# Seven-product stage, its first pairs: VectorE's order around pair one, and T1's low half on GpSimd

## The chip, the cores and the metric

The kernel runs on one core of one Trainium2 chip. The metric is the device time of one execution in microseconds. The engines are TensorE (PE in the profile; PEld is its weight load), VectorE (DVE), ScalarE (ACT), GpSimd (POOL) and SyncE (SP), which issues the loads.

## What is computed

Two layers of a decoder trunk on 512 tokens of width 1024, in float32. Each has token mixing (three branches), a LayerNorm, and then the stage that the change touches: a SwiGLU feed-forward network of hidden width 2816, together with a gate for an embedding of the layer.

```python
f_gate, f_up = jnp.split(x @ w_ffn_in, 2, axis=-1)
ffn = (jax.nn.silu(f_gate) * f_up) @ w_ffn_out
ple = jax.nn.sigmoid(x @ w_ple_gate) * (p_i @ w_ple_proj)
return layer_norm(ALPHA * x + ffn + ple, ln2_g, ln2_b)
```

## The kernel before

**Numbers in two parts.** Every product is made of three TensorE passes on a high and a low part of each operand (function `three`, lines 1234 to 1236): high by high, high weights by low tokens, low weights by high tokens. ScalarE makes a high part by rounding, and VectorE or GpSimd makes the low part by subtracting it from the unrounded value.

**Ahead of the stage.** Two of the 22 feed-forward blocks are multiplied directly, as four projection tiles (`T_R` to `T_R + 3`). GpSimd makes the low halves of the first three; that of the last is made by VectorE ("tile low", line 2133), which signals `r_low`. At line 753 GpSimd waits for `r_low` and adds one to `lo_ready`, the count on which SP's loads wait (line 600). "Hidden" (lines 2156 and 2159) is the product of the two projections of a block.

**Seven products.** For the other blocks, two weight blocks at a time, the product of a 2x2 block matrix of weights with a 2x2 block matrix of tokens (upper and lower half of the width, first and second 256 tokens) is made with seven multiplications in place of eight. There are 24 such pairs: pairs 0 to 3 belong to the embedding's gate, the others to the feed-forward network. The text calls pair index 1 "pair one" and index 2 "pair two". One multiplication is a *unit* of twelve matmuls on 128x256. Four need sums of weights (s1 to s4; VectorE's "sum1" to "sum4", lines 2175 to 2193), and four take sums of tokens, T1 to T4, which are the same for all pairs and made once in a layer: "t" on VectorE (lines 2141 and 2143), "t high" on ScalarE (line 1140), "t low" on VectorE (line 2148 for T1 and T3, line 2150 for T2 and T4). T1 is the difference of two blocks of x; in unit 7 (s1 of pair 0) it is needed first.

The units of the first pairs run in this order: 0 a11.0, 1 a12.0, 2 a11.1, 3 a12.1, 4 s3.0, 5 s2.0, 6 a22.0, 7 s1.0, 8 s3.1, 9 s4.0, 10 s2.1, 11 a22.1, 12 s1.1, 13 a11.2, 14 s3.2, 15 s4.1, 16 s2.2, 17 a12.2, 18 a22.2, 19 s1.2, 20 a11.3, 21 s3.3, 22 s4.2 (the number behind the point is the pair's index).

**What a pair's results pass through.** ScalarE copies intermediate results out of PSUM (m1, m7, u2), VectorE adds them to the accumulators (c11 line 2201, c21 line 2207, c22 line 2218). For pairs 0 to 3 ScalarE then takes a Tanh of each token half, and VectorE multiplies with the embedding's projection ("product first" and "product second", line 2228) and adds to the residual `u` ("low first" and "low second", line 2236). "Low second" signals `gated`. Unit a11 of pair j (from j = 2 on) waits for `gated` of pair j - 2, unit s3 for c21 of the pair before, s4 for c22 of its own pair, s2 for m1 of its own pair, and a11 of index 1 for both blocks' "hidden".

**What sets the order.** `ffn_steps` (line 263) gives each of ScalarE, VectorE and GpSimd a list of steps, each with a number, and sorts it; the numbers are counted in units, and an engine works through its list in order. A step that waits holds everything behind it on that engine. VectorE's low halves of unit i stand at i - 3.5, and its step "low" is line 2129. GpSimd makes the low halves of the units a11, a12 and a22 (line 757).

Of the kernel before, what the change touches and what calls it, by code (L numbers as in the profile page):

```python
# [19 lines left out]
ALU = mybir.AluOpType  # L20
ACT = mybir.ActivationFunctionType
F32 = mybir.dt.float32
# [234 lines left out]
R_BANKS = ((2, 3), (1, 4))  # L257
T3, T2, T4, T1 = 1, 2, 3, 0
T_MADE = {T1: 1, T3: 2, T2: 3, T4: 4}
T_HIGHS, T_LOWS = (T1, T3, T2, T4), (T3, T2, T1, T4)  # L260


def ffn_steps():

    act = [(-9.1, ("t high", T1)), (-9, ("t high", T3)), (-8.9, ("t high", T2)), (-8.8, ("gate", 0)), (-4.4, ("gate", 1)),
           (2.4, ("t high", T4)), (19, ("hidden high", 0)), (26, ("hidden high", 1))]
    dve = [(-9.1, ("t", T1)), (-9, ("t", T3)), (-8.95, ("t", T2)), (-8.9, ("tile low", T_R + 3)), (-8.8, ("t low", T3)),
           (-8.7, ("t low", T2)), (-8.6, ("hidden", 0)), (-6, ("sum3", 0)), (-4.6, ("sum1", 0)), (-4, ("sum2", 0)),
           (-3.9, ("sum4", 0)), (0.55, ("hidden", 1)), (1.6, ("t", T4)), (2.1, ("t low", T1)), (3.2, ("t low", T4)),
           (3.55, ("sum3", 1)), (3.6, ("sum1", 1)), (5.6, ("sum2", 1)), (1.55, ("c11", 0)), (10.5, ("c11", 1)),  # L270
           (20, ("hidden low", 0)), (27, ("hidden low", 1))]
    pool = []
    for i, (kind, j) in enumerate(FFN_UNITS):
        act.append((i - (6 if kind in ("a12", "a22") else 5) + 0.5, ("high", i)))
        if kind not in ("a11", "a12", "a22"):
            dve.append((i - 4 + 0.5, ("low", i)))
    for j in range(NS):
        at = {kind: UNIT_AT[(kind, j)] for kind in PRODUCT}
        late = 1 if j < NG else 0
        act += [(at["a11"] + 1, ("m1", j)), (at["s3"] + 1 if j else 3.45, ("m7", j)),  # L280
                (at["s2"] + 1 if j else 5.45, ("u2", j)),
                (at["a22"] + 2 if j < NG else at["a12"] + 2, ("th first", j)), (at["s4"] + 1, ("th second", j))]
        if j >= NG:
            act += [(at["a22"] + 3, ("high first", j)), (at["s4"] + 3, ("high second", j))]
        if j > 1:
            dve.append((at["a12"] + 1, ("c11", j)))
        dve += [(at["a22"] + 1 if j else 5.55, ("c21", j)), (at["s1"] + 1 if j else 6.45, ("c22", j)),
                (at["a22"] + 2 + late, ("product first", j)), (at["a22"] + 4, ("low first", j)),
                (at["s4"] + (1.6 if late else 2), ("product second", j)),
                (at["s4"] + (2.4 if late else 4), ("low second", j))]  # L290
        if j:
            dve.append((at["a11"] - 0.4 if j > 1 else at["s4"] - 8.4, ("sum4", j)))
        if j >= 2:
            dve.append((at["s2"] - 6, ("sum2", j)))
        pool += [(at[kind] - 5, ("low", at[kind])) for kind in ("a11", "a12", "a22")]
        if j >= 2:
            dve += [(at["a11"] - 6, ("sum3", j)), (at["a11"] - 4.4, ("sum1", j))]
    act += [(NU - 6 + 0.6, ("tile", 0)), (NU - 4 + 0.6, ("tile", 1)), (NU - 2 + 0.6, ("tile", 2))]
    return [sorted(steps, key=lambda step: step[0]) for steps in (act, dve, pool)]
# [63 lines left out]
def build(nc, x_t, ple_t, pos, freq, weights, params, out):  # L363
    with ExitStack() as ctx:
# [168 lines left out]
        raw2_loaded = [sem("raw2_loaded0"), sem("raw2_loaded1")]  # L533
        x_raw = sem("x_raw")
        r_low = sem("r_low")
        t_made, t_high, t_low = sem("t_made"), sem("t_high"), sem("t_low")
        unit_high, unit_low, unit_used = sem("unit_high"), sem("unit_low"), sem("unit_used")
        a11_low = sem("a11_low")
        sum1, sum3, sum2, sum4 = sem("sum1"), sem("sum3"), sem("sum2"), sem("sum4")
# [112 lines left out]
        def _(pool):  # L652
# [50 lines left out]
            for layer in range(L):  # L703
# [43 lines left out]
                tiles(layer, T_OUT, T_R)  # L747
                for t in range(T_R, T_S - 1):
                    low(t, first)
                pool.wait_ge(r_low, layer + 1)  # L750
                pool.wait_ge(lo_ready, first + (T_S - 1))
                for _ in range(1):
# [478 lines left out]
        def _(pe):  # L1231
# [268 lines left out]
            for layer in range(L):  # L1500
# [88 lines left out]
                def unit(i):  # L1589

                    kind, j = FFN_UNITS[i]
                    at = layer * NS + j
                    source, k0, token = PRODUCT[kind]
                    if kind in ("a12", "a22"):
                        arrived(T_S + TILE_UNIT_AT[(kind, j)], first)
                    elif kind == "a11":
                        pe.wait_ge(a11_low, at + 1)
                    else:
                        pe.wait_ge(unit_low, layer * NLOW + (LOW_UNIT_AT[(kind, j)] + 1))
                    if j == 0 and source == "t":  # L1600
                        pe.wait_ge(t_low, layer * 4 + (T_LOWS.index(k0) + 1))
                    if kind == "a11" and j == 1:
                        pe.wait_ge(ffn_s, layer * NR + NR)
                    elif kind == "a11" and j >= NG + 2:
                        pe.wait_ge(h_done, layer * FK + (NR + j - 2 - NG + 1))
                    elif kind == "a11" and j >= 2:
                        pe.wait_ge(gated, layer * NG + (j - 1))
                    elif kind == "s3":
                        if j == 0:
                            pe.wait_ge(ffn_s, layer * NR + 1)  # L1610
                        else:
                            pe.wait_ge(c21_ready, at)
                    elif kind == "s4":
                        pe.wait_ge(c22_ready, at + 1)
                    elif kind == "s2":
                        pe.wait_ge(m1_copied, at + 1)
                    elif kind == "a12":
                        if j == 0:
                            pe.wait_ge(ffn_s, layer * NR + 1)
                        else:  # L1620
                            pe.wait_ge(c11_ready, at)
                    elif kind == "a22":
                        pe.wait_ge(m7_copied, at + 1)
                    elif kind == "s1":
                        pe.wait_ge(u2_copied, at + 1)
                    bank = {"a12": B_BANK, "s3": E_BANK, "a22": E_BANK}.get(kind, A_BANK[j % 2])
                    onto = kind not in ("a11", "a12", "s3")
                    for k in range(KH):
                        if source == "x":
                            tok_h, tok_l = xh[:, k0 + k, token:token + HALF], xl[:, k0 + k, token:token + HALF]  # L1630
                        else:
                            tok_h, tok_l = t_hi[:, k0, k], t_lo[:, k0, k]
                        c = slice(k * P, k * P + P)
                        last = three(psum[:, bank, 0:HALF], ring(wh, i)[:, c], ring(wl, i)[:, c], tok_h, tok_l,
                                     k == 0 and not onto, k == KH - 1, onto)
                    last.then_inc(unit_used, 1)
# [740 lines left out]
```

## Time and profile before

| | |
|---|---|
| median of 3 runs | 1766.08 us (1764.22 to 1767.32) |
| the profiled execution | 1764.14 us, span 1762.3 us |
| TensorE busy | 1741.4 us (99%) |
| VectorE busy | 1268.4 us (72%) |
| ScalarE busy | 968.5 us (55%) |
| GpSimd busy | 892.2 us (51%) |
| granted TensorE clock, mean | 0.998 of full speed |

The shares are means over many stages. In a timeline row the first number is the start in us from the start of the span, the second the duration; a number in brackets at the end is the idle time of the engine just before, with what ended it. The stage stands twice in the trace; the rows below are of the first layer, where its first unit starts at 507.90 us.

### The profile page before, as it was taken

The numbers are of one execution on the slowest core, as the hardware profiler recorded it, in microseconds if no ns is written. First come the engines' busy times: TensorE is split into PE (matmuls) and PEld (weight loads), VectorE is DVE, ScalarE is ACT, GpSimd is POOL, SyncE is SP. The second block draws the span as 40 slices with busy tenths as digits, with TensorE's granted clock in tenths as the row PEclk, the third lists the DMA queues.
The fourth block names the chain that finished last, engine by engine and source line by source line (L and its number), as shares of the span: only waits on it lengthen the run. The fifth ranks groups of instructions, "written<-read, shape, count | busy, mean of one in ns | idle before, by whom it ended". The sixth has DMA issues, their size and how long they took to land.

```text
span 1762.3 us, 29278 instructions
## 1 busy us (share of the span) xinstructions
PE 1741.4 (99%) x10142; PEld 1532.9 (87%) x10142; DVE 1268.4 (72%) x2457; ACT 968.5 (55%) x1909; POOL 892.2 (51%) x522
## 2 busy tenths in 40 slices
PE   9999999999999999999999999999999999999997
PEld 8878888888789999988898788888887899999886
DVE  6279889877799888713363888897868998886033
ACT  4545887844466555522244558877445655655222
POOL 5446779654433343454434566895544343334542
PEclk9999999999999999999999999999999999999999
DMA  5334221223333223233223333212232323232331
GB/s 182 97 95 122 82 74 61 73 84 102 95 115 113 104 97 120 74 122 104 96 88 97 106 107 91 68 61 79 89 103 89 120 97 119 98 102 93 118 104 64
DMA packets 50411, 171.93 MB, mean 98 GB/s; under 512 B 6240, under 2 KB 6496, under 8 KB 50272
## 3 DMA queue, kind: packets, MB, share of 16 engines
q1 hardware_dynamic: 49408, 168.84, 30.2%
q8 instruction: 82, 1.34, 0.3%
q10 hardware_dynamic: 864, 1.28, 0.2%
q14 instruction: 57, 0.47, 0.1%
HBM read 162.76 MB, written 2.10 MB: 94 GB/s over the span
## 4 chain that ended last, share of the span: by engine, by line
PE 93%; DVE 4%; ACT 2%; issue 1%; DMA 0%; SPq 0%; DVEq 0%; ACTq 0%
PE banks L1234 25%; PE banks L1236 25%; PE banks L1235 25%; PE banks L1291 3%; PE banks L1293 3%; PE banks L1292 3%; PE banks L1403 2%; PE banks L1359 2%; DVE sb_xl L1936 1%; DVE sb_u L1929 1%; PE banks L1390 1%; DVE sb_u L1899 1%; PE banks L1383 1%; PE banks L1323 1%; PE banks L1384 1%
## 5 line engine op out<-in xcount | busy, mean ns | idle before, releaser
L669 POOL TENSOR_TENSOR sb_wl<-sb_wraw,sb_wh 128x1024 fp32r<-128x1024 f32 x205 | 497.6, 2431 | 500.3 <-ACT sb_wh L813 474.7
L1234 PE MATMUL banks<-sb_xh,sb_wh 128*128 128x512 f32 (+1 forms) x1152 | 403.7, 350 | 5.3 <-DVE sb_u L2236 3.5
L1236 PE MATMUL banks<-sb_xh,sb_wl 128*128 128x512 f32 (+1 forms) x1152 | 389.2, 338 | 0.0
L1235 PE MATMUL banks<-sb_xl,sb_wh 128*128 128x512 f32 (+1 forms) x1152 | 388.5, 337 | 0.0
L813 ACT ACTIVATE sb_wh<-sb_wraw 128x1024 fp32r<-128x1024 f32 x199 | 210.3, 1058 | 260.5 <-PE banks L1236 151.4
L1234 PEld LDWEIGHTS banks<-sb_xh,sb_wh 128*128 128x128 f32 x1152 | 219.1, 190 | 26.8 <-issue 7.1
L1236 PEld LDWEIGHTS banks<-sb_xh,sb_wl 128*128 128x128 f32 x1152 | 218.7, 190 | 24.2
L1235 PEld LDWEIGHTS banks<-sb_xl,sb_wh 128*128 128x128 f32 x1152 | 219.5, 191 | 14.1
L1234 PE MATMUL banks<-sb_t_hi,sb_wh 128*128 128x256 f32 x768 | 217.3, 283 | 0.0
L1235 PE MATMUL banks<-sb_t_lo,sb_wh 128*128 128x256 f32 x768 | 217.3, 283 | 0.0
L1236 PE MATMUL banks<-sb_t_hi,sb_wl 128*128 128x256 f32 x768 | 217.3, 283 | 0.0
L757 POOL TENSOR_TENSOR sb_wl<-sb_wraw,sb_wh 128x512 fp32r<-128x512 f32 x72 | 94.0, 1319 | 156.6 <-ACT sb_wh L1132 156.6
L1848 DVE TENSOR_TENSOR sb_u<-sb_u,banks 128x512 f32<-128x512 f32 x32 | 21.9, 686 | 197.1 <-PE banks L1236 197.1
L1234 PEld LDWEIGHTS banks<-sb_t_hi,sb_wh 128*128 128x128 f32 x768 | 147.5, 192 | 0.0
L1235 PEld LDWEIGHTS banks<-sb_t_lo,sb_wh 128*128 128x128 f32 x768 | 147.5, 192 | 0.0
L1236 PEld LDWEIGHTS banks<-sb_t_hi,sb_wl 128*128 128x128 f32 x768 | 147.5, 192 | 0.0
L1795 DVE SCALAR_TENSOR_TENSOR banks<-sb_hconv,sb_par,banks 128x512 f32<-128x512 f32 x192 | 142.5, 742 | 0.5
L1234 PE MATMUL banks<-sb_hh,sb_wh 128*128 128x512 f32 x352 | 137.8, 391 | 0.0
L1235 PE MATMUL banks<-sb_hl,sb_wh 128*128 128x512 f32 x352 | 137.0, 389 | 0.0
L1236 PE MATMUL banks<-sb_hh,sb_wl 128*128 128x512 f32 x352 | 137.0, 389 | 0.0
L757 POOL TENSOR_TENSOR sb_wl<-sb_wraw2b,sb_wh 128x512 fp32r<-128x512 f32 x48 | 62.1, 1294 | 90.8 <-ACT sb_wh L1132 90.8
L2129 DVE TENSOR_TENSOR sb_wl<-banks,sb_wh 128x512 fp32r<-128x512 f32 x144 | 98.4, 683 | 2.3 <-ACT sb_wh L1132 2.3
(353 smaller groups left out, 4085.9 us busy)
## 6 DMA issues: line engine op xcount, KB each, us to landing
sb_wraw<-in_weights SPq DMA_DIRECT2D x256, 512.0 KB, 3.5
sb_wraw2a<-in_weights SPq DMA_DIRECT2D x24, 512.0 KB, 3.6
sb_wraw2b<-in_weights SPq DMA_DIRECT2D x24, 512.0 KB, 4.5
sb_u<-in_x SPq DMA_DIRECT2D x8, 256.0 KB, 6.5
sb_q_raw<-sb_qn_t SPq DMA_DIRECT2D x16, 128.0 KB, 2.2
sb_k_raw<-sb_kn_t SPq DMA_DIRECT2D x16, 128.0 KB, 2.3
out<-sb_u SPq DMA_DIRECT2D x8, 256.0 KB, 2.1
sb_q_raw<-sb_qr_t SPq DMA_DIRECT2D x16, 64.0 KB, 2.0
```

Source lines behind the costliest of these rows:

```text
L669: nc.gpsimd.tensor_tensor(wl[:, t % WS, :], wraw[:, t % 2, :], wh[:, t % WS, :].bitcast(F32), ALU.subtract).then_inc(lo_ready, 1)
L757: nc.gpsimd.tensor_tensor(ring(wl, n), raw_unit(kind, j), ring(wh, n).bitcast(F32), ALU.subtract).then_inc(a11_low if kind == "a11" else l ...
L813: nc.scalar.activation(wh[:, t % WS, :], wraw[:, t % 2, :], ACT.Copy).then_inc(hi_ready, 1)
L1234: nc.tensor.matmul(out, wh_, xh_, start=start, stop=False, skip_group_check=onto)
L1235: nc.tensor.matmul(out, wh_, xl_, start=False, stop=False, skip_group_check=onto)
L1236: return nc.tensor.matmul(out, wl_, xh_, start=False, stop=stop, skip_group_check=onto)
L1291: nc.tensor.matmul(o, th_, h[:, kk], start=(k == 0), stop=False)
L1292: nc.tensor.matmul(o, th_, lw[:, kk], start=False, stop=False)
L1293: last = nc.tensor.matmul(o, tl_, h[:, kk], start=False, stop=(k == GROUP_K[name] - 1))
L1359: last = nc.tensor.transpose(psum[0:rows, bank, b * P:b * P + P], src, ident[:])
L1795: steps.done(v.scalar_tensor_tensor(acc, h, w, acc, ALU.mult, ALU.add))
L2129: v.tensor_tensor(ring(wl, n), raw_unit(kind, j), ring(wh, n).bitcast(F32), ALU.subtract).then_inc(unit_low, 1)
```

## The change

Three things change, and all stand in the head of the stage.

In VectorE's list for pair 0, "product second", "low first" and "low second" move up to stand right behind "product first". Pair one's c11, c21 and c22, the low half of unit 15 (s4.1) and the weight sum "sum2" of pair two follow in a new order.

T1's low half ("t low" of T1) leaves VectorE's list. GpSimd makes it, ahead of its wait at line 753, as soon as ScalarE has rounded T1; it signals a semaphore of its own, `t1_low`, for which the unit s1.0 waits.

The other token sums' semaphore `t_low` therefore counts three in a layer in place of four.

```diff
-T_HIGHS, T_LOWS = (T1, T3, T2, T4), (T3, T2, T1, T4)
+T_HIGHS, T_LOWS = (T1, T3, T2, T4), (T3, T2, T4)
...
-            dve.append((i - 4 + 0.5, ("low", i)))
+            dve.append((i - 4 + 0.5 if i != UNIT_AT[("s4", 1)] else 10.54, ("low", i)))
...
                 for t in range(T_R, T_S - 1):
                     low(t, first)
+                pool.wait_ge(t_high, layer * 4 + (T_HIGHS.index(T1) + 1))
+                nc.gpsimd.tensor_tensor(t_lo[:, T1], t_raw[:, T1], t_hi[:, T1].bitcast(F32), ALU.subtract).then_inc(t1_low, 1)
                 pool.wait_ge(r_low, layer + 1)
                 pool.wait_ge(lo_ready, first + (T_S - 1))
...
-                        pe.wait_ge(t_low, layer * 4 + (T_LOWS.index(k0) + 1))
+                        if k0 == T1:
+                            pe.wait_ge(t1_low, layer + 1)
+                        else:
+                            pe.wait_ge(t_low, layer * 3 + (T_LOWS.index(k0) + 1))
```

VectorE from "product first" of pair 0 to c22 of pair one, before (`banks` is PSUM; line 2228 is a product, 2236 an addition to `u`, 2187 a "sum2" and 2193 a "sum4", 2129 a low half, 2201, 2207 and 2218 are c11, c21 and c22):

```order
L2228 SCALAR_TENSOR_TENSOR banks<-banks,sb_pp 128x512
L2236 SCALAR_TENSOR_TENSOR sb_u<-sb_u,banks 128x2x256
L2187 TENSOR_TENSOR banks<-banks,sb_wraw 128x512
L2201 TENSOR_TENSOR banks<-banks,sb_m_126 128x256
L2129 TENSOR_TENSOR sb_wl<-sb_wl_raw,sb_wh 128x512
L2228 SCALAR_TENSOR_TENSOR banks<-banks,sb_pp 128x512
L2236 SCALAR_TENSOR_TENSOR sb_u<-sb_u,banks 128x2x256
L2129 TENSOR_TENSOR sb_wl<-banks,sb_wh 128x512
L2207 SCALAR_TENSOR_TENSOR banks<-banks,sb_u_128 128x256
L2129 TENSOR_TENSOR sb_wl<-banks,sb_wh 128x512
L2193 TENSOR_TENSOR banks<-banks,sb_wraw 128x512
L2218 SCALAR_TENSOR_TENSOR banks<-banks,sb_m_127 128x256
```

And now (lines stand six further down):

```order
L2234 SCALAR_TENSOR_TENSOR banks<-banks,sb_pp 128x512 x2
L2242 SCALAR_TENSOR_TENSOR sb_u<-sb_u,banks 128x2x256 x2
L2135 TENSOR_TENSOR sb_wl<-sb_wl_raw,sb_wh 128x512
L2207 TENSOR_TENSOR banks<-banks,sb_m_126 128x256
L2213 SCALAR_TENSOR_TENSOR banks<-banks,sb_u_128 128x256
L2135 TENSOR_TENSOR sb_wl<-banks,sb_wh 128x512
L2193 TENSOR_TENSOR banks<-banks,sb_wraw 128x512
L2224 SCALAR_TENSOR_TENSOR banks<-banks,sb_m_127 128x256
L2135 TENSOR_TENSOR sb_wl<-banks,sb_wh 128x512
L2199 TENSOR_TENSOR banks<-banks,sb_wraw 128x512
```

Both products and both additions stand first; "sum2" of pair two has gone from the third place to the ninth instruction, and c22 ahead of the last low half.

GpSimd from the last projection tiles to its first units, before (line 669 is a tile's low half, 757 a unit's):

```order
L669 TENSOR_TENSOR sb_wl<-sb_wraw,sb_wh 128x1024 x3
L757 TENSOR_TENSOR sb_wl<-sb_wraw,sb_wh 128x512 x2
L757 TENSOR_TENSOR sb_wl<-sb_wraw2b,sb_wh 128x512
L757 TENSOR_TENSOR sb_wl<-sb_wraw2a,sb_wh 128x512
L757 TENSOR_TENSOR sb_wl<-sb_wraw,sb_wh 128x512
```

And now:

```order
L670 TENSOR_TENSOR sb_wl<-sb_wraw,sb_wh 128x1024 x3
L752 TENSOR_TENSOR sb_t_lo<-sb_t_raw,sb_t_hi 128x1024
L760 TENSOR_TENSOR sb_wl<-sb_wraw,sb_wh 128x512 x2
L760 TENSOR_TENSOR sb_wl<-sb_wraw2b,sb_wh 128x512
L760 TENSOR_TENSOR sb_wl<-sb_wraw2a,sb_wh 128x512
```

T1's low half stands between the tiles' and the units' low halves, ahead of the signal to the loads.

## Rows read from the trace of the kernel before

**Rows 1.** The page, part 1: busy time, share of the span, instructions.

```profile
PE 1741.4 (99%) x10142; PEld 1532.9 (87%) x10142; DVE 1268.4 (72%) x2457; ACT 968.5 (55%) x1909; POOL 892.2 (51%) x522
```

**Rows 2.** Waits of TensorE, whole span: us in total, times, longest.

```profile
PE banks L1234 <- DVE sb_u L2236: 3.5, 2, 1.7
```

**Rows 3.** Timeline, TensorE, unit 12 to 13: start, us, line, names, idle before.

```profile
526.49 0.28 PE L1236 MATMUL banks<-sb_t_hi,sb_wl 128*128 128x256 f32 x1
528.52 0.36 PE L1234 MATMUL banks<-sb_xh,sb_wh 128*128 128x256 f32 x1 [1.75 <-DVE sb_u L2236]
```

**Rows 4.** Timeline, VectorE, around unit 13.

```profile
523.96 0.69 DVE L2228 SCALAR_TENSOR_TENSOR banks<-banks,sb_pp 128x512 f32<-128x512 f32 x1
524.75 0.69 DVE L2236 SCALAR_TENSOR_TENSOR sb_u<-sb_u,banks 128x512 f32<-128x512 f32 x1
525.35 0.69 DVE L2187 TENSOR_TENSOR banks<-banks,sb_wraw 128x512 f32<-128x512 f32 x1
...
527.68 0.69 DVE L2236 SCALAR_TENSOR_TENSOR sb_u<-sb_u,banks 128x512 f32<-128x512 f32 x1
...
529.22 0.68 DVE L2129 TENSOR_TENSOR sb_wl<-banks,sb_wh 128x512 fp32r<-128x512 f32 x1
```

**Rows 5.** Timeline, ScalarE, the same stretch.

```profile
522.96 0.59 ACT L1170 ACTIVATE banks<-banks 128x512 f32<-128x512 f32 x1
...
526.14 0.60 ACT L1132 ACTIVATE sb_wh<-banks 128x512 fp32r<-128x512 f32 x1 [1.81 <-DVE banks L2187]
526.63 1.14 ACT L1132 ACTIVATE sb_wh<-sb_wraw 128x512 fp32r<-128x512 f32 x2
```

**Rows 6.** Timeline, GpSimd and VectorE, a few units later.

```profile
527.33 2.52 POOL L757 TENSOR_TENSOR sb_wl<-sb_wraw,sb_wh 128x512 fp32r<-128x512 f32 x2 [3.85 <-ACT sb_wh L1132]
...
533.25 1.24 DVE L2180 TENSOR_TENSOR banks<-sb_wraw2b,sb_wraw2a 128x512 f32<-128x512 f32 x1
```

**Rows 7.** Timeline, VectorE's c22 of pair two and TensorE's unit 22.

```profile
540.01 0.42 DVE L2218 SCALAR_TENSOR_TENSOR banks<-banks,sb_m 128x256 f32<-128x256 f32 x1
...
541.54 0.28 PE L1234 MATMUL banks<-sb_xh,sb_wh 128*128 128x256 f32 x1
```

**Rows 8.** Timeline, ScalarE and VectorE, the token sums.

```profile
496.82 1.05 ACT L1140 ACTIVATE sb_t_hi<-sb_t_raw 128x1024 fp32r<-128x1024 f32 x1
...
497.33 1.22 DVE L2141 TENSOR_TENSOR sb_t_raw<-sb_u,sb_t_raw 128x1024 f32<-128x1024 f32 x1
498.48 1.22 DVE L2133 TENSOR_TENSOR sb_wl<-sb_wraw,sb_wh 128x1024 fp32r<-128x1024 f32 x1
...
512.47 1.21 DVE L2148 TENSOR_TENSOR sb_t_lo<-sb_t_raw,sb_t_hi 128x1024 fp32r<-128x1024 f32 x1
...
512.58 1.06 ACT L1140 ACTIVATE sb_t_hi<-sb_t_raw 128x1024 fp32r<-128x1024 f32 x1 [2.66 <-DVE sb_t_raw L2143]
```

**Rows 9.** Timeline, GpSimd and VectorE in earlier stages.

```profile
401.52 2.43 POOL L669 TENSOR_TENSOR sb_wl<-sb_wraw,sb_wh 128x1024 fp32r<-128x1024 f32 x1 [2.17 <-ACT sb_wh L813]
401.62 2.88 DVE L2062 TENSOR_TENSOR sb_gb<-sb_gb,sb_ga 128x512 f32<-128x512 f32 x1
...
125.53 3.05 POOL L669 TENSOR_TENSOR sb_wl<-sb_wraw,sb_wh 128x1024 fp32r<-128x1024 f32 x1 [2.49 <-ACT sb_wh L813]
```

**Rows 10.** TensorE, SP's waits, ScalarE and VectorE ahead of unit 2.

```profile
502.46 0.39 PE L1234 MATMUL banks<-sb_xh,sb_wh 128*128 128x512 f32 x1
...
SPq L600 <- POOLq L753: 7.1, 1, 7.1
...
506.09 0.63 ACT L1132 ACTIVATE sb_wh<-sb_wraw2b 128x512 fp32r<-128x512 f32 x1 [0.90 <-DMA sb_wraw2b<-in_weights]
...
507.79 1.26 DVE L2129 TENSOR_TENSOR sb_wl<-sb_wl_raw,sb_wh 128x512 fp32r<-128x512 f32 x1 [1.48 <-ACT sb_wh L1132]
...
509.68 0.69 DVE L2159 TENSOR_TENSOR sb_th<-sb_th,banks 128x512 f32<-128x512 f32 x1
...
510.77 0.28 PE L1234 MATMUL banks<-sb_xh,sb_wh 128*128 128x256 f32 x1
```

More of the change, by code:

```diff
@@ L268, in ffn_steps @@
            (-8.7, ("t low", T2)), (-8.6, ("hidden", 0)), (-6, ("sum3", 0)), (-4.6, ("sum1", 0)), (-4, ("sum2", 0)),
-           (-3.9, ("sum4", 0)), (0.55, ("hidden", 1)), (1.6, ("t", T4)), (2.1, ("t low", T1)), (3.2, ("t low", T4)),
-           (3.55, ("sum3", 1)), (3.6, ("sum1", 1)), (5.6, ("sum2", 1)), (1.55, ("c11", 0)), (10.5, ("c11", 1)),
+           (-3.9, ("sum4", 0)), (0.55, ("hidden", 1)), (1.6, ("t", T4)), (3.2, ("t low", T4)),
+           (3.55, ("sum3", 1)), (3.6, ("sum1", 1)), (5.6, ("sum2", 1)), (1.55, ("c11", 0)), (10.51, ("c11", 1)),
            (20, ("hidden low", 0)), (27, ("hidden low", 1))]
@@ L286, in ffn_steps @@
             dve.append((at["a12"] + 1, ("c11", j)))
[L287 to L290, printed above, removed]
+        dve += [({0: 5.55, 1: 10.52}.get(j, at["a22"] + 1), ("c21", j)),
+                ({0: 6.45, 1: 10.58}.get(j, at["s1"] + 1), ("c22", j)),
+                (at["a22"] + 2 + late, ("product first", j)), (at["a22"] + 4 if j else 9.5, ("low first", j)),
+                (at["s4"] + (1.6 if late else 2) if j else 9.3, ("product second", j)),
+                (at["s4"] + (2.4 if late else 4) if j else 9.7, ("low second", j))]
         if j:
@@ L293, in ffn_steps @@
         if j >= 2:
-            dve.append((at["s2"] - 6, ("sum2", j)))
+            dve.append((at["s2"] - 6 if j > 2 else 10.56, ("sum2", j)))
         pool += [(at[kind] - 5, ("low", at[kind])) for kind in ("a11", "a12", "a22")]
@@ L535, in build @@
         r_low = sem("r_low")
-        t_made, t_high, t_low = sem("t_made"), sem("t_high"), sem("t_low")
+        t_made, t_high, t_low, t1_low = sem("t_made"), sem("t_high"), sem("t_low"), sem("t1_low")
         unit_high, unit_low, unit_used = sem("unit_high"), sem("unit_low"), sem("unit_used")
```

## The prediction

> **What bounds the kernel now.** I read the page first: TensorE is busy for 99% of the span [rows 1], so only a stretch in which it stands still, or starts late, can change the time. The view of its waits, next, shows how little of that there is: the longest entry is 3.5 us in two waits, one in each layer, for VectorE's line 2236 [rows 2]. Line 2236 with the second token half is "low second", which signals `gated`; unit 13 of the stage (a11 of pair two) may not start without it. TensorE's timeline shows one such wait: the last matmul of unit 12 started at 526.49, the next could have started 0.12 us later, and it started at 528.52 after an idle stretch of 1.75 us [rows 3]. With the slower first matmuls behind it this costs about 1.95 us in a layer, 3.9 us in both. No edit to the order around pair one can win more than that.
>
> VectorE is the engine waited for. From 523.96 its rows follow each other without an idle entry [rows 4]; two independent operations on 512 columns start 0.60 us apart (524.75 and 525.35). So what is moved ahead moves something else back by as much. That is why the later waits matter: the last TensorE start that hangs on this row of work is unit 22 (s4 of pair two), at 541.54, and what it needs, c22 of pair two, ended at 540.01 + 0.42 = 540.43 [rows 7]. The hand-over from VectorE to TensorE took 0.15 us at the wait itself (527.68 + 0.69 = 528.37 to 528.52) [rows 3, 4]. Unit 22 thus had 541.54 - 540.58 = 0.96 us to spare. However early TensorE gets away at unit 13, it is stopped there again unless VectorE itself is earlier: **0.96 us, not 1.95, is the most that a new order can keep in a layer.**
>
> **The moved operations of pair one.** In the new order "product first", "product second", "low first" and "low second" follow each other from 523.96 at 0.60 us each. The Tanh that "product second" needs ended at 522.96 + 0.59 = 523.55 on ScalarE [rows 5], so it does not hold it. "Low second" starts at 525.76 and ends at 526.45 in place of 528.37, 1.92 us earlier. With 0.15 us for the hand-over TensorE is released at 526.60, when it is ready (526.61): the wait goes.
>
> What was put back is late next. The weight sum "sum2" of pair two started at 525.35 [rows 4]; in the new order it comes behind three 0.60 us operations (the other product and both additions take the place of one), the low half of s3, two 0.34 us copies of c11 and c21, and the low half of s4, and ends near 528.9, 2.9 us later. ScalarE waits for just that result (1.81 us idle before its row at 526.14) and has two more roundings (1.14 us for both), a Tanh and the copy of m1 queued behind it [rows 5]. At some 0.55 us each, from 529.0, m1 is copied by about 531.4. Unit 16 wants it at 526.61 + 3 x 1.44 = 530.93 (1.44 us is twelve matmuls at 0.12 us), so TensorE waits 0.5 to 0.6 us there. The low half that VectorE takes of this sum, at 529.22 before, must now wait for ScalarE until 529.6 (+0.4). And GpSimd's two low halves that started at 527.33 [rows 6] start near 530.2 and end near 532.8, across VectorE's weight sum "sum3" of pair three, which reads SBUF twice. By the blocking shown below this costs up to 1.3 us, less the 0.56 us that the sum at 533.25 (1.24 us, where 0.68 is usual) lost to GpSimd before and then no longer loses [rows 6]. VectorE reaches c22 of pair two some 0.8 us later than before, so unit 22 starts at 541.4 in place of 541.54. I take 0.1 us won in a layer from the new order; the ends are 0.96 us won and 0.4 us lost.
>
> **T1's low half.** The operation removed from VectorE takes 1.21 us at 512.47, but VectorE's next one needs T4's rounding, which ScalarE ends at 512.58 + 1.06 = 513.64 [rows 8], where the removed one ended at 513.68. Removing it gives VectorE nothing but an idle microsecond. What matters is where the operation goes. GpSimd is free then, and gets it when T1 is rounded, at 496.82 + 1.05 = 497.87. VectorE is at that moment inside T2 (497.33 for 1.22 us), and the low half of the last projection tile is next (498.48 to 499.70) [rows 8]; both have two SBUF inputs.
>
> How these two engines share SBUF is seen elsewhere in this trace: a GpSimd subtraction of the same size asked at 401.52 while a two-input VectorE operation ran; it was done by 403.95, and VectorE's following two-input operation, 0.68 us long when alone, took 2.88 us, from 401.62 until 0.55 us after GpSimd's end [rows 9]. That is 2.2 us lost. Where GpSimd asked as late as 0.2 us before VectorE's operation ended, VectorE's next one went first and GpSimd took 3.05 us [rows 9]. Here it asks at about 497.95, 0.6 us ahead of 498.55, so I take the first pattern: the tile's low half ends at 501.9, not 499.7. The Trainium skill, SBUF — State Buffer, section "Who interferes with whom", has it as a lock: a VectorE instruction with two SBUF inputs and a GpSimd one that reads SBUF block each other fully, and issue order decides who waits. The trace agrees, with 2.2 us for a 2.43 us instruction; the page's "whole instruction" would make it 2.4 us and the sum below 0.4 us larger.
>
> Three things hang on that low half. TensorE's projection of the tile started at 502.46 [rows 10]; 501.9 and 0.15 are still in time. GpSimd's signal at line 753 waits for it, and SP's load of the pair's second weight tile waits for line 753 (7.1 us) [rows 10], with the loads of pair one queued behind it. These loads are late by the same 2.2 us, since nothing else holds them: ScalarE stood 0.90 us for them at 506.09, and VectorE then 1.48 us for ScalarE at 507.79 [rows 10]. So VectorE's idle time does not absorb the delay; it moves with it. "Hidden" of the second block ended at 509.68 + 0.69 = 510.37 and ends at 512.57. Unit 2 (a11 of pair one), which waits for it, started at 510.77 [rows 10] and starts at 512.72: 1.95 us lost, and about 0.1 us more for the restart, as at unit 13.
>
> **Sum.** In each layer + 2.05 + 0.1 for VectorE, which stays the later of the two by that much, - 0.1 for the new order: 2.05 us; two layers, 4.1 us. The profiled execution took 1764.14 us (span 1762.3) and would take 1768.2. It lies 1.94 us under the median of the three runs, 1766.08, so the forecast on that scale is **1770.2 us**. The bounds for T1's move are 0 (GpSimd runs where VectorE reads PSUM) and 2.4 us plus 0.4 if the projection is held too; with the order's bounds a layer lies between -0.96 and +3.2.
>
> **The rivals.**
> 1. *T1's low half costs nothing and VectorE is relieved.* For it: 1.21 us leave an engine whose rows show no idle entry for long [rows 4]. Against it: VectorE's operations at 497.33 and 498.48 both read SBUF twice [rows 8], and its time at 512.47 was not on the path. The order's 0.1 us a layer is left: 1765.9. The Trainium skill, Perfetto Trace Analysis, section "Optimizing Scalar/DVE Operations", leaves both open: with a saturated VectorE moving work may pay, and between these two engines it might not, since they share a port.
> 2. *The tile's low half goes first, T1's behind it* (the 3.05 us pattern). Line 753 and the loads are then on time; the 2.2 us fall on the operations behind, where VectorE's idle 1.48 us takes part, and collisions with GpSimd's first four low halves give some back. "Hidden" would be 0.7 to 1.7 us late against 0.25 us of slack: 0.5 to 1.5 us a layer, near 1768.
> 3. *Faster.* T1 is free, and GpSimd's late low halves miss the sum of pair three: the 0.96 us of unit 22 are kept twice, 1764.2. To pass 0.2% a layer would have to win 1.8 us, which needs VectorE earlier at c22 than the trace has it.
> 4. *Slower still.* The tile's low half comes after 502.3 and holds the projection as well: from that point each microsecond counts fully; 0.5 us more in a layer, 1771.3.
>
> **How the numbers follow.** The forecast 0.62 (own range 1768.6 to 1771.5), rival 1 0.15, rival 2 0.10, rival 3 0.05, rival 4 0.08. A measurement here tells about 0.2%, 3.5 us, from no change: 1762.6 and 1769.6 are the lines. Of the forecast some 0.45 lies above the upper, with rival 4 0.53 slower; rival 3 passes the lower line in 0.03; the rest, 0.44, is the same. The range, 1765.6 to 1771.8, takes in rivals 1 and 2 and the upper part of 4.
>
> **What would show it.** Right: in the profile after, GpSimd's new row near 498 for 2.4 to 2.9 us, the tile's low half on VectorE near 3.4 us long in place of 1.22, line 753's signal near 501.9, a TensorE wait of 1.5 us or so for "hidden" at the stage's third unit, none at unit 13, and waits of about half a microsecond for m1 and for c22 of pair two. Wrong: the tile's low half still 1.2 us long, or TensorE without a wait at the third unit, or c22 of pair two earlier than now against unit 13.

## The result, and the profile after

The changed kernel takes 1768.38 us (median of 22 runs, 1768.00 to 1771.75), the kernel before in as many runs beside it 1765.78 us: a ratio of 1.0018, 95% interval 1.0012 to 1.0024. The change makes the kernel slower by 0.18%, clear of zero but under the 0.2% from which the prediction counted a change; by its own lines this is "the same". The forecast of 1770.2 us was 1.8 us too high: its own range, 1768.6 to 1771.5, missed the time by 0.2 us, and the whole range, 1765.6 to 1771.8, holds it. The profiled execution of the changed kernel took 1768.49 us (span 1766.7), which is 4.35 us more than that of before; the working had said 4.1 between these two.

In the trace after, line numbers above 750 are three higher on GpSimd, ScalarE and TensorE (753 is 756, 1234 is 1237), six higher on VectorE (2129 is 2135, 2228 is 2234, 2236 is 2242) and one higher on SP (600 is 601); those of the experiments lie in between. The page's first line, to be held against [rows 1]:

```profile
PE 1743.1 (99%) x10142; PEld 1532.8 (87%) x10142; DVE 1268.2 (72%) x2455; ACT 967.0 (55%) x1909; POOL 899.1 (51%) x524
```

Busy times tell nothing: two instructions went from VectorE to GpSimd, and the engines are as busy as before. The waits of TensorE tell it (us in total, times, longest):

```profile
PE banks L1237 <- DVE sb_th L2165: 2.7, 2, 1.3
...
PE banks L1237 <- DVE banks L2224: 1.2, 2, 0.6
PE banks L1237 <- ACT sb_m L1154: 1.2, 2, 0.7
...
PE banks L1237 <- POOL sb_wl L760: 0.5, 2, 0.3
```

The entry of [rows 2], 3.5 us for the second addition of pair one, is gone. Four others stand in its place, each twice, once in a layer. The timeline of TensorE, layer one, at units 0, 2, 13, 16 and 22 gives the starts:

```profile
508.54 0.39 PE L1237 MATMUL banks<-sb_xh,sb_wh 128*128 128x256 f32 x1 [0.21 <-POOL sb_wl L760]
...
513.01 0.36 PE L1237 MATMUL banks<-sb_xh,sb_wh 128*128 128x256 f32 x1 [1.33 <-DVE sb_th L2165]
...
528.92 0.35 PE L1237 MATMUL banks<-sb_xh,sb_wh 128*128 128x256 f32 x1
...
533.91 0.36 PE L1237 MATMUL banks<-sb_t_hi,sb_wh 128*128 128x256 f32 x1 [0.44 <-ACT sb_m L1154]
...
543.63 0.36 PE L1237 MATMUL banks<-sb_xh,sb_wh 128*128 128x256 f32 x1 [0.61 <-DVE banks L2224]
```

TensorE's starts in the two traces of before and after, set side by side, give what each unit lost (+) or won against the one listed above it, in us. The start of the program, long before the change, adds 0.3 us that belongs to the execution and not to the kernel.

| unit | layer one | layer two | waits for |
|---|---|---|---|
| 0 | +0.37 | +0.46 | GpSimd's first low half |
| 2 | +1.60 | +1.59 | "hidden" of the second block |
| 13 | -1.84 | -1.85 | nothing any more |
| 16 | +0.60 | +0.88 | m1 of pair two |
| 21 | +0.25 | +0.25 | c21 of pair two, and the slower restart in unit 16 |
| 22 | +0.83 | +0.84 | c22 of pair two |
| sum | +1.81 | +2.17 | |

Where the first two lines come from stands in the timelines of GpSimd and VectorE and in SP's waits:

```profile
498.24 2.88 POOL L752 TENSOR_TENSOR sb_t_lo<-sb_t_raw,sb_t_hi 128x1024 fp32r<-128x1024 f32 x1 [5.78 <-ACT sb_t_hi L1143]
...
497.63 1.23 DVE L2147 TENSOR_TENSOR sb_t_raw<-sb_u,sb_t_raw 128x1024 f32<-128x1024 f32 x1
498.77 3.42 DVE L2139 TENSOR_TENSOR sb_wl<-sb_wraw,sb_wh 128x1024 fp32r<-128x1024 f32 x1
...
SPq L601 <- POOLq L756: 18.6, 2, 9.3
```

GpSimd takes T1's low half at 498.24, while VectorE is inside T2; VectorE's low half of the projection tile, 1.22 us in [rows 8], takes 3.42 and ends at 502.19. SP then waits 9.3 us for GpSimd's signal in place of the 7.1 us of [rows 10], and the loads behind it are 2.2 us late.

### The profile page after: what moved, and what is told of

Read it like the earlier page. It is cut to its first block and busy times, and to the rows that moved or that the text cites. A ratio compares the mean times of both kernels' runs of the same rounds, so it can differ in the third digit from the quotient of the medians.

```text
span 1766.7 us, 29278 instructions
## 1 busy us (share of the span) xinstructions
PE 1743.1 (99%) x10142; PEld 1532.8 (87%) x10142; DVE 1268.2 (72%) x2455; ACT 967.0 (55%) x1909; POOL 899.1 (51%) x524
```

## The experiments

Ten kernels were run, nine of them 7 to 11 times each, beside fresh runs of the kernel before. What is compared first is the trace, unit by unit; the medians follow.

### The order alone

```diff
-T_HIGHS, T_LOWS = (T1, T3, T2, T4), (T3, T2, T4)
+T_HIGHS, T_LOWS = (T1, T3, T2, T4), (T3, T2, T1, T4)
...
-                nc.gpsimd.tensor_tensor(t_lo[:, T1], t_raw[:, T1], t_hi[:, T1].bitcast(F32), ALU.subtract).then_inc(t1_low, 1)
```

> The changed kernel with T1's low half back on VectorE, behind T2's (line 269 keeps the step "t low" of T1 and its key 2.1): the new order around pair one alone, the whole result computed. **Theory (the shared lock is the cost):** the order pays back what it takes. The wait of 1.95 us at unit 13 goes, and TensorE waits instead about 0.6 us at unit 16 for ScalarE's m1 and 0.6 to 0.7 us in all at units 21 and 22 for c21 and c22 of pair two; VectorE's add sum3 of pair two runs into GpSimd's lows and takes 1.5 us instead of 0.7, as it did in the changed kernel, and that is what makes c22 late. Net per layer between -0.7 and +0.1 us; median 1764.4 to 1766.0 us, 0 to -1.4 us against the kernel before. **Rival A (the order is the cost, T1's move is free):** the wait is given back in full and more; the kernel is as slow as the changed one, 1768.4 us. **Rival B (the order wins outright):** -1.9 us per layer with nothing new late at units 16 to 22; 1762.0 us.

Measured: 1764.38 us (1764.06 to 1764.87), ratio 0.9989 (0.9980 to 0.9998). TensorE's waits:

```profile
PE banks L1235 <- DVE banks L2219: 1.2, 2, 0.6
PE banks L1235 <- ACT sb_m L1152: 1.2, 2, 0.7
```

Against the trace of before, unit 13 starts 1.9 us earlier in each layer, and units 16, 21 and 22 give back 0.61 + 0.25 + 0.84 us in layer one and 0.88 + 0.24 + 0.84 in layer two. The order is worth nothing in the trace: 1764.24 us for the profiled execution, 1764.14 for that of before. Rivals A and B both fall. But the median is 1.5 us lower than before's, more than the trace explains; that difference is taken up below.

### T1's low half alone

```diff
+                pool.wait_ge(t_high, layer * 4 + (T_HIGHS.index(T1) + 1))
+                nc.gpsimd.tensor_tensor(t_lo[:, T1], t_raw[:, T1], t_hi[:, T1].bitcast(F32), ALU.subtract).then_inc(t1_low, 1)
```

> The kernel before with nothing but T1's low half moved to GpSimd, at line 751, ahead of the signal of line 753; VectorE's order around pair one is as before. The whole result is computed. **Theory (the shared lock is the cost):** VectorE's low half of the last token tile, ready to begin at 498.5 us, is held by GpSimd's add and ends near 502.2 instead of 499.7 us; through the semaphore of line 753 the loads into the token tile come 2.2 to 2.5 us later, hidden half 1 follows, and TensorE waits at unit 2 for it for 1.3 us more; unit 0 loses 0.3 to 0.4 us to GpSimd's first low half. The wait of 1.95 us at unit 13 stays, as a wait of about 1.9 us. Sum +1.6 to +2.3 us per layer, median 1769.0 to 1770.4 us, so slower than the changed kernel or level with it. **Rival A (T1's move is free or a relief to VectorE):** level with the kernel before, 1765.8 us or up to 1.2 us under it. **Rival B (T1's delay is absorbed by the wait at unit 13):** that wait shrinks from 1.95 to 0.3 us and the sum is +0.4 per layer, 1766.6 us.

Measured: 1770.24 us (1768.28 to 1771.75), ratio 1.0020 (1.0011 to 1.0029); the profiled execution 1768.28, 4.14 us over that of before. VectorE's row, then TensorE's waits:

```profile
498.55 3.42 DVE L2138 TENSOR_TENSOR sb_wl<-sb_wraw,sb_wh 128x1024 fp32r<-128x1024 f32 x1
```

```profile
PE banks L1236 <- DVE sb_u L2241: 3.6, 2, 1.8
PE banks L1236 <- DVE sb_th L2164: 2.7, 2, 1.3
...
PE banks L1236 <- POOL sb_wl L759: 0.5, 2, 0.3
```

Unit 0 is 0.37 and 0.42 us late, unit 2 another 1.59 in each layer, and the wait at unit 13 stays as it was: VectorE and TensorE are late by the same amount, so that wait takes nothing up. The theory holds; in the trace rival A is over 4 us off and rival B, with its 0.8 us for both layers, over 3. In the trace the two parts add: 0.1 for the order and 4.1 for T1 make 4.2, and the changed kernel's difference is 4.35.

### T1's low half behind the signal

```diff
-                pool.wait_ge(t_high, layer * 4 + (T_HIGHS.index(T1) + 1))
-                nc.gpsimd.tensor_tensor(t_lo[:, T1], ...).then_inc(t1_low, 1)
...
+                pool.wait_ge(t_high, layer * 4 + (T_HIGHS.index(T1) + 1))
+                nc.gpsimd.tensor_tensor(t_lo[:, T1], ...).then_inc(t1_low, 1)
```

The two lines move from ahead of the wait and signal of line 753 to right behind them.

> The changed kernel with T1's low half on GpSimd issued behind the signal of line 753 instead of ahead of it: GpSimd still does it at nearly the same time, but the loads into the token tile no longer wait for it in GpSimd's queue. The whole result is computed. **Theory 1 (what costs is GpSimd holding the memory that both engines use, whoever is next on VectorE):** the signal waits for the low half of the token tile, which now ends near 499.7 us, so the loads are on time and GpSimd's op begins right behind, at about 499.8 us; it then meets VectorE's next work (the first sums and lows of the stage) and the hidden half is late by 1 to 1.5 us by that road; TensorE waits at unit 2 for 1.0 to 1.4 us more than in the kernel before, unit 0 not at all. Per layer +1.0 to +1.5 with the order's 0 to -0.6: median 1766.6 to 1768.6 us. **Theory 2 (only the late signal of line 753 costs):** the loads are back at their time, hidden half 1 with them, unit 2 waits no longer than in the kernel before, and the median is that of the order alone, 1764.4 to 1766.0 us.

Measured: 1767.71 us (1766.76 to 1769.05), ratio 1.0009 (1.0000 to 1.0018). SP's wait, GpSimd's and VectorE's timelines, and TensorE's wait:

```profile
SPq L601 <- POOLq L754: 14.2, 2, 7.1
```

```profile
500.11 3.19 POOL L756 TENSOR_TENSOR sb_t_lo<-sb_t_raw,sb_t_hi 128x1024 fp32r<-128x1024 f32 x1 [7.74 <-POOLq L754]
```

```profile
498.69 1.22 DVE L2139 TENSOR_TENSOR sb_wl<-sb_wraw,sb_wh 128x1024 fp32r<-128x1024 f32 x1
499.83 1.22 DVE L2154 TENSOR_TENSOR sb_t_lo<-sb_t_raw,sb_t_hi 128x1024 fp32r<-128x1024 f32 x1
500.96 3.42 DVE L2156 SCALAR_TENSOR_TENSOR sb_t_lo<-sb_t_raw,sb_t_hi 128x1024 fp32r<-128x1024 f32 x1
...
506.23 1.78 DVE L2186 TENSOR_TENSOR banks<-sb_wraw 128x512 f32<-128x512 f32 x1
```

```profile
PE banks L1237 <- DVE sb_th L2165: 2.6, 2, 1.3
```

The signal is back at its time (7.1 us a layer, as in [rows 10]), the tile's low half takes 1.22 us again, and still TensorE waits 1.3 us at unit 2, which starts 1.47 us later than before. The 2.2 us have only moved on to VectorE's next operation, T2's low half: 3.42 us for 1.22. The idle 1.48 us that VectorE had ahead of 507.79 [rows 10] take up a part of them, and a weight sum that now runs beside GpSimd's first low halves, 1.78 us for 0.69, gives a part back. Theory 2 falls: the late signal is one road from the blocked operation to unit 2, not the cause. What the better place does save is unit 0, and some 0.5 us a layer in all.

### T1's low half 13 us later

```diff
+                    if n == UNIT_AT[("a22", 0)]:
+                        pool.wait_ge(t_high, layer * 4 + (T_HIGHS.index(T1) + 1))
+                        nc.gpsimd.tensor_tensor(t_lo[:, T1], ...).then_inc(t1_low, 1)
```

> The changed kernel with T1's low half on GpSimd behind the low half of unit 6, about 13 us later than in the changed kernel, when the loads, the tile's low half and the hidden half are long done. The whole result is computed; the operand is used first by a unit that comes later. **Theory (the place is the cost, not the engine):** the loads, hidden half 1 and units 0 and 2 are at the times of the kernel before; GpSimd's add of 2.4 us there holds VectorE's low of T4 by up to 1 us, and c21 of pair zero after it, so unit 8 waits some 0.3 us. Per layer +0.3 and the order's 0 to -0.6: median 1765.0 to 1766.6 us, level with the kernel before. **Rival (GpSimd is the wrong engine anywhere, its 2.4 us against VectorE's 1.2 us come back as a wait wherever it stands):** unit 8 or one of the next waits 1.2 us or more per layer, 1768 us or over.

Measured: 1766.30 us (1765.61 to 1766.61), ratio 1.0002 (0.9993 to 1.0011). GpSimd, VectorE and TensorE:

```profile
511.89 3.39 POOL L762 TENSOR_TENSOR sb_t_lo<-sb_t_raw,sb_t_hi 128x1024 fp32r<-128x1024 f32 x1
...
514.14 2.22 DVE L2157 SCALAR_TENSOR_TENSOR sb_t_lo<-sb_t_raw,sb_t_hi 128x1024 fp32r<-128x1024 f32 x1 [1.13 <-ACT sb_t_hi L1144]
...
519.19 0.36 PE L1238 MATMUL banks<-sb_t_hi,sb_wh 128*128 128x256 f32 x1 [0.64 <-ACT sb_u L1165]
```

Units 0 and 2 start as in the kernel before. The theory's size is right and its unit is wrong: T4's low half loses 1.00 us (2.22 for 1.22), the weight sum behind it comes later, ScalarE's rounding of that sum holds its copy of u2, and unit 7 waits and starts 0.79 us later in layer one and 0.80 in layer two, not unit 8 by 0.3. The cost of T1 on GpSimd falls from 2.1 to 0.9 us a layer by its place alone; at none of the three places did it become a gain, since the 1.2 us that it takes from VectorE were not on the path.

### Before once more, and one sum moved

The trace of before left two things open: why the order alone has a lower median than its trace gives, and what holds VectorE ahead of unit 13. The runs of before fall into three groups, 1.6 us apart, and each run's granted TensorE clock goes with them, in all but two of 74 runs (0.998 at 1766.38 and 1766.45 us, times of the middle group). All 22 runs of the two experiments without a long wait of TensorE, 1 and 4, kept 0.998.

> The kernel before once more, unchanged, for its trace. The 33 runs of it beside the first four experiments fall into three groups: ten at 1763.9 to 1764.7 us with a granted clock of 0.998 or 0.999, fifteen at 1765.5 to 1766.7 us, nearly all at 0.997, and eight at 1767.2 to 1768.0 us at 0.996 or 0.997; the trace at hand, 1764.14 us, is of the lowest. **Theory (the clock falls at the wait of 1.95 us before unit 13, in some executions, in one layer or in both):** if this execution is of a higher group, 1765.5 us or more, its trace shows TensorE's granted clock below 1.00 in the stretch behind unit 13 of one layer (two for 1767 and more), and 1.6 us more per layer there. **Rival:** the clock is 1.00 there and the time is lost elsewhere. An execution of the lowest group, 1763.9 to 1764.7 us, tells nothing on this.

It ran once, in 1764.64 us: the lowest group, which tells nothing on the clock. Its waits are those of before. What it does show is how far two executions of one kernel stand apart at the same clock: 0.5 us, all at the start of the program.

The second kernel changes one number in `ffn_steps`:

```diff
-            dve += [(at["a11"] - 6, ("sum3", j)), (at["a11"] - 4.4, ("sum1", j))]
+            dve += [(at["a11"] - 6 if j > 2 else 5.57, ("sum3", j)), (at["a11"] - 4.4, ("sum1", j))]
```

> The kernel before with one VectorE step moved: the weight sum sum3 of pair two goes from behind sum4 of pair one to behind c21 of pair zero, five places up. In the old place it meets GpSimd's low halves and runs 1.5 us; in the new one it does not. The whole result is computed. **Theory (VectorE's chain ahead of unit 13 is what TensorE waits for, and the length of that wait decides on the clock):** the wait at unit 13 falls from 1.95 to about 0.9 us in both layers and nothing else gets late: -0.9 us per layer, 1762.3 us for an execution with the clock at 0.998, and as no wait is as long as 1.9 us all runs lie in one group: median 1762.0 to 1762.8 us, 3.0 to 3.8 us under the median before. **Rival 1 (the groups do not come from that wait):** three groups as before, each 1.8 us lower, median 1764.0 us. **Rival 2 (sum3's time is not on the path):** unit 13 waits as before, 1765.9 us.

Measured: 1762.48 us (1762.02 to 1763.99), ratio 0.9981 (0.9972 to 0.9990). VectorE's row for the moved sum, and TensorE's wait at unit 13:

```profile
518.59 0.68 DVE L2175 TENSOR_TENSOR sb_wl_raw<-sb_wraw 128x512 f32<-128x512 f32 x1
```

```profile
PE banks L1234 <- DVE sb_u L2236: 1.8, 2, 0.9
```

The sum takes 0.68 us in its new place; in the old one it had taken 1.18, not the 1.5 that was expected. The wait is halved, from 1.75 us [rows 3] to 0.9. Unit 13 starts 0.80 and 0.90 us earlier in the two layers and nothing gives it back. The median falls by 3.3 us where the trace, 1760.6 against 1762.3 us of span, falls by 1.7. Rival 2 is out. Ten of the eleven runs have a granted clock of 0.998 and end by 1763.2; one, 1763.99, has 0.997. So of rival 1's three groups two are all but gone.

### The new order, mended

```diff
-            dve.append((at["s2"] - 6 if j > 2 else 10.56, ("sum2", j)))
+            dve.append((at["s2"] - 6 if j > 2 else 10, ("sum2", j)))
```

> The new order of the changed kernel with T1's low half on VectorE, as in the first experiment, and the weight sum sum2 of pair two put right behind pair one's second addition instead of behind c21 of pair one (its key 10 in place of 10.56). The whole result is computed. **Theory (the order gives its gain back because sum2 is put three places too late):** high half 16 on ScalarE, m1 of pair two, c21 and c22 of pair two are on time again: the waits at units 16, 21 and 22 go, unit 14 waits some 0.4 us for c21 of pair one. Net per layer about -1.3 us, median 1761.2 to 1762.0 us. **Rival (the wait moves on whatever the place: VectorE has no room in this stretch):** a wait of 0.6 us or more shows up again at units 13 to 22 in another place and the time is that of the first experiment, 1764.4 us.

Measured: 1761.35 us (1761.17 to 1761.86), ratio 0.9976 (0.9966 to 0.9986). The waits at units 16, 21 and 22 are gone, and one new entry is left, 0.35 us at unit 14 for c21 of pair one:

```profile
PE banks L1235 <- DVE banks L2208: 0.4, 2, 0.2
```

The rival falls. The give-back of the new order was no law of a full engine; it came from one step, "sum2" of pair two, put behind four operations, c11 and c21 of pair one and two low halves. With it ahead of them only c21 comes too late, by 0.35 us.

> The two moves together: the new order with sum2 of pair two right behind pair one's second addition, and sum3 of pair two behind c21 of pair zero; T1's low half on VectorE. The whole result is computed. **Theory:** no wait of TensorE over 0.1 us is left between units 8 and 40 of either layer, -1.9 us per layer against the trace of before: 1760.2 to 1761.0 us, all runs in one group, 4.8 to 5.6 us under the median before. **Rival (VectorE is near full here, a new collision with GpSimd's low halves takes the gain):** one of units 13 to 22 waits 0.5 us or more, 1761.5 to 1763 us.

This kernel has both edits, that of "sum2" and that of "sum3". Measured: 1760.88 us (1760.14 to 1761.17), ratio 0.9971 (0.9960 to 0.9982), the fastest of all here, 4.9 us under the kernel before and 7.5 under the changed one. The two stretches that held the wait at unit 13, in the trace of before and then in this one (length, then busy us and instructions of TensorE, its weight loads, VectorE, ScalarE and GpSimd, then granted clock, DMA share and GB/s):

```profile
526.00:545.00 19.00, 17.25 (x144) 17.08 (x143) 18.83 (x32) 11.99 (x25) 7.67 (x6) 1.00 0.33 114
1400.00:1420.00 20.00, 18.25 (x153) 18.08 (x152) 19.83 (x33) 13.01 (x27) 7.68 (x6) 1.00 0.32 107
```

```profile
526.00:545.00 19.00, 19.00 (x161) 19.00 (x160) 18.93 (x33) 13.17 (x27) 7.80 (x6) 1.00 0.35 120
1400.00:1420.00 20.00, 20.00 (x169) 20.00 (x169) 19.93 (x35) 13.66 (x28) 10.28 (x8) 1.00 0.31 107
```

TensorE, busy for 17.25 of 19 and 18.25 of 20 us before, does not stand still any more. The bound that the prediction gave for any order, 0.96 us a layer, does not hold: this order wins 1.97, and that of the seventh experiment won 1.49 and 1.39.

### A longer wait, and the sum of both parts

```diff
-                (at["s4"] + (2.4 if late else 4), ("low second", j))]
+                (at["s4"] + (2.4 if late else 4) if j else 12.55, ("low second", j))]
```

> The kernel before with VectorE's second addition of pair one moved three steps later, behind the low half of unit 16: the wait at unit 13 is made longer on purpose, from 1.95 to about 3.3 us. The whole result is computed. **Both theories:** the work alone is 1.3 to 1.5 us longer per layer, so an execution with the granted clock at 0.998 takes 1766.8 to 1767.4 us. **Theory (a longer wait at unit 13 lets the granted clock fall more often):** in the kernel before 17 of 54 runs kept their clock, with the wait at 0.9 us ten of eleven did, without it all; here fewer than 3 in 10 do, most runs are 1.6 us (one layer) or 3.2 us (both) above, 1768.5 to 1770.5 us, and the median is 1768.5 us or more. If the traced execution is one of them, the clock is below 1.00 right behind unit 13. **Rival (the groups have nothing to do with the length of this wait):** the share of the groups stays, about a third at the lowest, half 1.6 us above and a sixth 3.2 us above; the median is 1768.5 us too, and only the shares and the trace tell.

Measured: 1769.90 us (1767.92 to 1771.15), ratio 1.0024 (1.0015 to 1.0034). No run of ten has a granted clock of 0.998; two have 0.997, eight 0.996. The profiled execution is one of the two, and shows the thing itself. TensorE waits 3.07 us at unit 13 in both layers (6.1 us in two waits). In the first the clock stays; in the second it falls. The stretches by granted clock (third column from the end), layer one and layer two, each from the idle time on:

```profile
526.00:529.30 3.30, 0.30 (x3) 0.10 (x1) 3.30 (x7) 1.90 (x4) 2.42 (x2) 1.00 0.01 2
529.30:533.30 4.00, 3.92 (x33) 3.95 (x34) 3.55 (x7) 1.65 (x4) 0.07 (x1) 1.00 0.56 185
...
1401.00:1404.20 3.20, 0.32 (x3) 0.12 (x1) 3.20 (x7) 2.19 (x4) 2.03 (x2) 1.00 0.01 3
1404.20:1408.20 4.00, 3.81 (x20) 3.84 (x21) 2.81 (x7) 0.88 (x2) 0.47 (x1) 0.59 0.58 174
1408.20:1412.00 3.80, 3.80 (x33) 3.80 (x33) 2.22 (x5) 2.11 (x5) 1.30 (x1) 0.98 0.25 97
```

and TensorE's rows in layer two:

```profile
1404.39 0.36 PE L1234 MATMUL banks<-sb_xh,sb_wh 128*128 128x256 f32 x1 [3.07 <-DVE sb_u L2236]
...
1404.94 0.40 PE L1235 MATMUL banks<-sb_xl,sb_wh 128*128 128x256 f32 x1
1405.14 0.42 PE L1236 MATMUL banks<-sb_xh,sb_wl 128*128 128x256 f32 x1
1405.36 0.42 PE L1234 MATMUL banks<-sb_xh,sb_wh 128*128 128x256 f32 x1
...
1408.35 0.29 PE L1236 MATMUL banks<-sb_t_hi,sb_wl 128*128 128x256 f32 x1
```

From 1404.94 to 1408.35 matmuls start 0.21 us apart in place of 0.12, with the clock at the lower of its two levels (1.2 in place of 2.4 GHz); 16 starts at 0.09 us more each cost 1.5 us. That is the distance between the groups. The runs with a granted clock of 0.998 or more, by the longest idle time of TensorE in units 0 to 22:

| kernels | longest idle time | runs that kept 0.998 |
|---|---|---|
| experiments 1, 4, 6, 7, 8 | 0.9 us or less | 48 of 49 |
| the changed kernel, experiments 3 and 10 | 1.3 us | 37 of 44 |
| the kernel before | 1.75 us | 26 of 74 |
| experiment 2, with both waits | 1.79 us | 5 of 11 |
| this one | 3.07 us | 0 of 10 |

The rival, that the shares stay, falls. The length of the wait does not settle it alone: of the three kernels with 1.3 us the changed one kept its clock in 18 of 22 runs, experiment 3 in 8 of 11 and experiment 10 in all 11.

> The changed kernel, T1's low half on GpSimd ahead of the signal of line 753, with the two weight sums where the eighth experiment has them (sum2 of pair two behind pair one's second addition, sum3 behind c21 of pair zero). The whole result is computed. **Theory (the costs add: T1's low half on GpSimd costs the start of the stage, whatever VectorE's order is later):** against the eighth experiment unit 0 is 0.3 to 0.5 us and unit 2 another 1.6 us later in each layer, and no unit behind makes it good: +3.9 to +4.2 us, 1764.3 to 1765.0 us where the clock stays at 0.998. **Rival (the late start gives VectorE and GpSimd slack, and the good order then costs less than the sum):** unit 13 and those behind it start no more than 1.2 us late per layer, 1763.2 us or less.

Measured: 1764.81 us (1764.15 to 1765.08), ratio 0.9994 (0.9985 to 1.0003); the profiled execution 1764.37, 3.93 us over that of the eighth experiment, although the start of the program was 0.3 us shorter. Against that trace units 0 and 2 are 0.54 and 1.59 us late in layer one, 0.33 and 1.60 in layer two, and no unit behind waits; of the changed kernel's waits in the stage that for "hidden" and that for GpSimd's first low half are left:

```profile
PE banks L1237 <- DVE sb_th L2165: 2.7, 2, 1.3
...
PE banks L1237 <- POOL sb_wl L760: 0.5, 2, 0.4
```

The costs add. T1's low half costs 2.0 to 2.2 us a layer at the start of the stage, also with the better order of VectorE behind it; the rival falls.

## Why the prediction came out as it did

**The wait at unit 13 and what follows it.** Right. The two products came one behind the other at 526.30 and the two additions at 527.50, late by the 2 us that VectorE was late, and the wait went. VectorE's rows from there to c22:

```profile
526.30 1.28 DVE L2234 SCALAR_TENSOR_TENSOR banks<-banks,sb_pp 128x512 f32<-128x512 f32 x2
527.50 1.27 DVE L2242 SCALAR_TENSOR_TENSOR sb_u<-sb_u,banks 128x512 f32<-128x512 f32 x2
...
534.10 1.52 DVE L2181 TENSOR_TENSOR sb_wl_raw<-sb_wraw2b,sb_wraw2a 128x512 f32<-128x512 f32 x1
...
536.86 0.70 DVE L2186 TENSOR_TENSOR banks<-sb_wraw2b,sb_wraw2a 128x512 f32<-128x512 f32 x1
...
543.06 0.42 DVE L2224 SCALAR_TENSOR_TENSOR banks<-banks,sb_m 128x256 f32<-128x256 f32 x1
```

What gives it back is what the working named: m1 at unit 16 (0.60 and 0.88 us; 0.5 to 0.6 was said), and c22 at unit 22. The collision of "sum3" of pair three with GpSimd's two low halves is there, 1.52 us for 0.68, and the sum at 536.86 is free of it, as forecast, in place of the 1.24 us of [rows 6]. The 0.25 us up to unit 21 were not in the working; they are a part of the same delay: c21 ended at 541.21, and the unit started 0.15 us later, at 541.36. Net -0.16 and +0.12 us in the two layers, where 0.1 won was taken.

**T1's low half.** Right in place, road and size. The tile's low half ended at 502.19 (501.9 was said; the program's start adds 0.3), 3.42 us long, and did not hold the projection; 2.05 us were forecast up to unit 2, and units 0 and 2 together lost 1.97 and 2.05. One thing on the road was not named: the late loads also hold GpSimd's first low half, so 0.4 us of it fall at unit 0 already. Of the lock the Trainium skill, SBUF — State Buffer, section "Who interferes with whom", says that the port pair which both engines share is an exclusive lock, and that issue order decides who blocks. The traces agree: the VectorE operation that followed lost 2.20 us in the changed kernel and in the third experiment (3.42 for 1.22) and 1.00 us in the fourth, where it came only 1.14 us ahead of GpSimd's end, and in all three it ended 1.07 or 1.08 us after GpSimd's row, which is nearly its own length.

**The sum against the profile, and then the median.** The sum, 1764.14 + 4.1 = 1768.2 us for a profiled execution, was 0.3 us off, the 0.3 us of the program's start. The last step failed: "on that scale" I added 1.94 us, the distance of the profiled execution from the median, as if that belonged to every kernel. It does not. In about two of three executions of the kernel before (48 of 74) the granted clock falls, in 15 of them twice by their times, for 1.5 to 1.6 us each, and the experiments that shorten, remove or lengthen the wait of 1.75 us at unit 13 tie the fall to it; the traced executions happened to be free of it. The change takes that wait away and has one of 1.3 us at unit 2 instead, and most of the extra is gone: 18 of its 22 runs lie within 0.5 us of 1768.5, the other four, at 1770.6 to 1771.75 us with a clock of 0.996 or 0.997, pay. So the median moved by 2.6 us and the trace by 4.35. In the kernel with T1's part alone, which keeps the wait, the medians move by 4.4 and the traces by 4.14. The term that was mis-sized is this one: it should have been about zero (the changed kernel's median lies 0.1 us under its profiled execution). With it went the chances, which put "slower" (0.53) ahead of "the same" (0.44). The fall itself was caught only in the trace with the longer wait; that it is the same in the kernel before rests on the run times, their distance and the clock that each run reports, not on a trace. Why one execution keeps its clock and the next does not is open.

**The bound on any order.** The prediction said that 0.96 us is the most that a new order can keep in a layer, since TensorE is stopped at unit 22 "again unless VectorE itself is earlier". VectorE could be. Two of its sums ahead of unit 13 ran into GpSimd in the trace of before, which I had not looked at:

```profile
520.49 1.29 POOL L757 TENSOR_TENSOR sb_wl<-sb_wraw2b,sb_wh 128x512 fp32r<-128x512 f32 x1 [9.03 <-ACT sb_wh L1132]
522.00 1.48 POOL L757 TENSOR_TENSOR sb_wl<-sb_wraw,sb_wh 128x512 fp32r<-128x512 f32 x1 [0.22 <-ACT sb_wh L1132]
...
521.15 1.18 DVE L2175 TENSOR_TENSOR sb_wl_raw<-sb_wraw 128x512 f32<-128x512 f32 x1
...
522.97 1.08 DVE L2180 TENSOR_TENSOR banks<-sb_wraw 128x512 f32<-128x512 f32 x1
```

Moving the first of them ahead of four operations freed both (0.68 and 0.70 us) and gave 0.80 to 0.90 us back. Even without that the seventh experiment passed the bound: its c22 of pair two ended at 539.51 in place of 540.43.

```profile
532.89 0.70 DVE L2181 TENSOR_TENSOR banks<-sb_wraw2b,sb_wraw2a 128x512 f32<-128x512 f32 x1
...
539.09 0.42 DVE L2219 SCALAR_TENSOR_TENSOR banks<-banks,sb_m 128x256 f32<-128x256 f32 x1
```

The sum at 533.25 missed GpSimd there (0.70 us for the 1.24 of [rows 6]), and each product and its addition, 0.79 and 0.80 us apart in the order of before, no longer follow each other directly: in the new order all four start 0.60 us apart. The prediction had reckoned with both in its working and left them out of its bound. Time lost to a collision looks like busy time in a row without idle entries; I read that row as full, and it was not. The chance of 0.03 for faster was right for this change, but the reason given for it was too strong.

**Rivals.** T1 at no cost, and with it the way to "faster": refuted by the second experiment, 4.1 us in the trace. The tile's low half first: refuted by the row of 3.42 us; the third experiment puts the two in that order, and T1 then costs 1.5 us a layer, the upper end of the 0.5 to 1.5 given. Slower still, by holding the projection: the low half ended at 502.19, and TensorE's rows from 501.82 on follow each other without an idle entry.

## What to carry to other kernels

Before moving an elementwise operation from VectorE to GpSimd, look at what VectorE runs at that moment: if it is one with two SBUF inputs, the next such operation may stand still for most of GpSimd's. Here that added up to 2.2 us for a subtraction of 2.43 us, and the 1.2 us taken off VectorE elsewhere did not pay for it. When steps are moved ahead on a full engine, ask for each step put back when its reader needs it; here one weight sum put behind four others gave back nearly all of 1.9 us a layer, and ahead of them 0.4. And a wait of TensorE of 1.75 us cost more than its length in two of three executions: compare the run times with the profiled execution before a difference between traces is added to a median.

## What the runs showed of the hardware that I had not expected

After 3.07 us of standing still TensorE's granted clock fell in one layer and not in the other of one execution, 0.6 us after the restart, and came back 3.4 us later. A blocked operation shows no idle entry, on either engine: the waiting is inside its duration. GpSimd's rows for T1's low half, 2.88, 3.19 and 3.39 us in three kernels where the same subtraction took 2.43 in [rows 9], end with VectorE's 3.42, 3.42 and 2.22 us behind them.
